# Turning the exponentials ahead of the new scores in the sixteen-pair attention

## The reference, cut to what matters

```
s = jnp.einsum('bqghd,bkgd->bghqk', qi, k_win).astype(jnp.float32) * scale
s = s - slopes * (t[:, None] - sp[None, :]).astype(jnp.float32)
p = masked_softmax(s, wmask)
o_win = jnp.einsum('bghqk,bkgd->bqghd', p.astype(dtype), v_win)
...
return g[..., 0:1] * o_cmp + g[..., 1:2] * o_slc + g[..., 2:3] * o_win
```

## Time and profile before

| | |
|---|---|
| time, median of 3 runs | 1466.04 us (1464.92 to 1466.94) |
| the profiled execution: time, span | 1466.22 us, 1464.4 us |
| PE busy | 1404.9 us (96%) |
| PEld, DVE, ACT, POOL busy | 1102.1, 593.2, 611.8, 626.4 us |
| mean granted TensorE clock | 0.988 |
| the sixteen-pair attention | about 558 to 703 us of the span |

### The profile page before, as it was taken

One profiled execution on the slowest core, in us unless ns is written; L12 is line 12 of the kernel. 1 busy time (PEld: TensorE's weight loads), 2 busy tenths in 40 slices (PEclk: granted clock), 3 DMA queues, 4 the chain that ended last, 5 costly groups with the idle time before them and its releaser, 6 DMA issues.

```text
span 1464.4 us, 19696 instructions
## 1 busy us (share of the span) xinstructions
PE 1404.9 (96%) x7313; PEld 1102.1 (75%) x7313; DVE 593.2 (41%) x1130; ACT 611.8 (42%) x1155; POOL 626.4 (43%) x345
## 2 busy tenths in 40 slices
PE   6999999999999999999999998898999999999999
PEld 5787887678778786666786687785788888888887
DVE  1104103732362244777343777978322332332000
ACT  4212222734123237888353665356343443443110
POOL 2763543564346523332335662520134444434441
PEclk9999999999999998999999999999999999999999
DMA  7553532012225420112123231102022323233230
GB/s 197 118 99 90 115 102 77 2 38 86 81 79 171 116 72 1 34 41 81 58 72 132 73 108 57 59 8 108 30 87 86 100 86 100 90 96 93 94 115 29
DMA packets 78399, 120.25 MB, mean 82 GB/s; under 512 B 8448, under 2 KB 41392, under 8 KB 77936
## 3 DMA queue, kind: packets, MB, share of 16 engines
q1 hardware_dynamic: 76096, 114.21, 26.9%
q0 software_dynamic: 2208, 4.98, 1.2%
q10 hardware_dynamic: 16, 0.00, 0.0%
HBM read 114.95 MB, written 4.19 MB: 81 GB/s over the span
## 4 chain that ended last, share of the span: by engine, by line
PE 77%; issue 8%; POOL 5%; DVE 3%; ACT 3%; DMA 2%; DVEq 1%; POOLq 1%; SPq 0%; ACTq 0%
PE psum L1685 20%; PE psum L1687 20%; PE psum L1686 20%; POOL weight_low L495 4%; PE psum L1734 3%; PE psum L1717 3%; PE psum L1697 3%; PE psum L1664 1%; PE psum L1845 1%; PE psum L2048 1%; PE psum L2024 1%; PE psum L1832 1%; ACT pair_probs L785 1%; POOL rstd L519 1%; DVEq L1412 1%
## 5 line engine op out<-in xcount | busy, mean ns | idle before, releaser
L495 POOL TENSOR_TENSOR weight_low<-weight_raw,weight_high 128x1024 fp32r<-128x1024 f32 x188 | 459.3, 2447 | 612.9 <-ACT weight_high L715 312.8
L1685 PE MATMUL psum<-act_ring,weight_high 128*128 128x512 f32 x704 | 282.8, 402 | 0.4 <-issue 0.4
L1687 PE MATMUL psum<-act_ring,weight_low 128*128 128x512 f32 x704 | 277.5, 394 | 0.0
L1686 PE MATMUL psum<-act_ring,weight_high 128*128 128x512 f32 x704 | 277.2, 394 | 0.0
L715 ACT ACTIVATE weight_high<-weight_raw 128x1024 fp32r<-128x1024 f32 x104 | 109.9, 1060 | 387.8 <-PE psum L1687 378.8
L1685 PE MATMUL psum<-weight_high,act_ring 128*128 128x512 f32 x480 | 193.4, 403 | 2.9 <-DVE odd_k L1292 2.3
L1687 PE MATMUL psum<-weight_high,act_ring 128*128 128x512 f32 x480 | 190.2, 396 | 0.0
L1686 PE MATMUL psum<-weight_low,act_ring 128*128 128x512 f32 x480 | 190.1, 396 | 0.0
L1685 PEld LDWEIGHTS psum<-act_ring,weight_high 128*128 128x128 f32 x704 | 132.6, 188 | 35.8 <-issue 5.2
L1687 PEld LDWEIGHTS psum<-act_ring,weight_low 128*128 128x128 f32 x704 | 132.4, 188 | 33.9
L1686 PEld LDWEIGHTS psum<-act_ring,weight_high 128*128 128x128 f32 x704 | 132.6, 188 | 30.7
(11 more groups left out here) (357 smaller groups left out, 2115.7 us busy)
## 6 DMA issues: line engine op xcount, KB each, us to landing
weight_raw<-in_w_ffn_in SPq DMA_DIRECT2D x88, 256.0 KB
weight_raw<-in_even_w_in SPq DMA_DIRECT2D x32, 512.0 KB
weight_raw<-in_w_in SPq DMA_DIRECT2D x24, 512.0 KB
weight_raw<-in_w_ffn_out SPq DMA_DIRECT2D x22, 512.0 KB
weight_raw<-in_odd_w_in SPq DMA_DIRECT2D x20, 512.0 KB
weight_raw<-in_even_w_out SPq DMA_DIRECT2D x8, 512.0 KB
weight_raw<-in_odd_w_in SPq DMA_DIRECT2D x16, 256.0 KB
weight_raw<-in_odd_w_out SPq DMA_DIRECT2D x8, 512.0 KB
```

Source lines behind the costliest of these rows:

```text
L495: nc.gpsimd.tensor_tensor(WL[:, r], RAW[:, r], WH[:, r].bitcast(f32), ALU.subtract).then_inc(split_ready, 1)
L1685: mm(bank, hi_l, hi_r, start=start, stop=False, skip_group_check=True)
L1686: mm(bank, hi_l, lo_r, start=False, stop=False, skip_group_check=True)
L1687: return mm(bank, lo_l, hi_r, start=False, stop=stop, skip_group_check=True)
```

## The change

In the loop of the sixteen-pair attention TensorE issues the turn of step u-2, with the one wait for `cmp_taken` that stands ahead of the first turn, before the scores of step u and no longer behind them. Nothing is added or taken away, and no other engine's order changes. The other two attentions of the kernel keep the old order.

```diff
             for u in range(ODD_UNITS + 4):
                 s = FOX_UNITS + u
+                if u == 2:
+                    pe.wait_ge(sem("cmp_taken"), 2 * NT)
+                if 2 <= u < ODD_UNITS + 2:
+                    pair_turn(s - 2)
                 if u < ODD_UNITS:
...
                     pair_scores(s, [part[:, 2 + q, :] for part in O_S], [part[:, b, :] for part in O_S])
-                if u == 2:
-                    pe.wait_ge(sem("cmp_taken"), 2 * NT)
-                if 2 <= u < ODD_UNITS + 2:
-                    pair_turn(s - 2)
                 if u >= 4 and u % 2 == 0:
```

## The result

The median of the changed kernel is 1509.9 us (1508.7 to 1510.1, four runs) and that of the kernel before, taken beside it, 1465.6: a ratio of 1.030 with a 95% interval of 1.028 to 1.032. The forecast was 1502.5 with a range of 1491 to 1517. The span of the profiled execution is 1508.2 us against 1464.4, so there are 43.8 us to place.

The account below looks back on a forecast made before the run. The stage was taken as bound by TensorE's amount of work. Loop stalls 33.2, first pair 2.0 and longer half-clock spell 1.2 sum to 36.4 us on 1466.22, forecast 1502.5; own range 1497 to 1509, 8 in 10 1491 to 1517.

Parts of the forecast that it names:

- The serial loop: Sixteen-pair attention: scores, DVE's maximum, copy of step s-2, turn, next scores; 2.25 us more a pair, 10.70 not 8.45.
- kind 0: Step with maximum 256 wide, copy 512: wait 1.36 us, 8 value matmuls cover 0.80, stall 0.56.
- kind 1: Step with maximum 128 wide, copy 384: wait 1.11 us, nothing for TensorE to do, stall 1.11.
- kind 3: Step with maximum 384 wide, copy 128: wait 1.10 us as measured, the back covers 0.52, stall 0.58.
- kind 2: Step with maximum 512 wide, copy 256: wait 1.37 us, 16 value matmuls take 1.67, no stall.
- The late back: Kind 3: back waits for ACT's pair copy, starts about 0.5 us late, ends about 1.04 behind scores, under the 1.10.
- The sign of failure: Forecast called wrong if, in kind 3, the back's wait for line 766 is the later one.
- The granted clock should stay 1.00 after the first pair: Stage's clock: no half clock beyond the start; only a longer first spell, taken as 1.2 us.
- rival 1: Clock falls in the stalls: 1.5 us lost per spell, 1515, 1527 or about 1600 us in all; chance 0.16.
- Is another engine late next? No.: Stage's other engines: DVE needs 6.3 us and ACT 7.0 a pair, both far under 10.7, so neither is late.
- Rival 2: Wait for the copy is shorter than summed, or only kind 1 stalls (18.7 us): time 1485; chance 0.10.
- Rivals 3 and 4: Turn ahead fills idle time, 2.2 us at most, 1464 (chance 0.02); or change does nothing, 1466 (chance 0.03).

Follow-up runs that it names:

- Experiment 1: Changed kernel, but in this stage DVE copies step s-2 ahead of the maximum of step s: 1476.9 us, ratio 1.007.
- experiment 4: Changed kernel plus 2, 4 and 2 products of zeros in steps of kind 0, 1 and 3, filling TensorE's idle places: 1502.0 us, ratio 1.025.
- Experiment 3: Changed kernel, but only head 1, whose bank ACT empties, is turned ahead of the scores, head 0 behind them: 1482.3 us, ratio 1.011.
- Experiment 7: Turn moved ahead of the scores only in steps of kind 3, otherwise the order of the kernel before: 1476.2 us, ratio 1.007.
- first version of the kernel before: Kernel before plus 5 and 8 products of zeros behind the scores of steps 0 and 1 of the sixteen-pair attention: 1465.9 us, ratio 0.9997.

## Why the prediction was right, and where it was off

**The serial loop.** Shown. The sum of maximum, copy and turn was right for each kind: from the end of the scores to the next turn it is 1.37 in kind 0 (1.36 forecast), 1.11 in kind 1 (1.11), 1.11 in kind 3 (1.10), and in kind 2 the values cover it. (The end is the next weight load in kind 0; in kinds 1 and 3, where TensorE idles, it is an estimate, the scores' first weight load plus their 0.48 and 0.72 of the earlier trace rows.) Experiment 1 cuts the loop at the one place that the forecast named, DVE's order, and 1.68 of the 2.22 us a pair go. With no more time at half clock than before, the stage costs 35.6 us more (experiment 4), against 33.2 + 2.0 forecast.

**The late back.** "About 0.5 late" was 0.52: it starts at 604.40 and the scores end at 603.88. It lies under the 1.11 as forecast, but only just: with its 0.52 of the earlier trace rows the back could end at 604.92, the copy ends at 604.87, and the turn starts at 604.99. The sign of failure that the prediction named, line 766 as the later wait in kind 3, stayed off by 0.07 us, and the chain even goes through line 766 there. So in kind 3 two paths end together. Some of the idle time also stands at another place than forecast: the waits view of TensorE's matmuls in the stage has 29.3 us ahead of line 1717 (its four rows added up, 33 forecast) and 6.0 ahead of line 1743.

**The clock.** Here the prediction was off, and by nearly all of the 7.4 us. "The granted clock should stay 1.00 after the first pair" is wrong: there are three spells in the pairs behind it. This is rival 1 in its mild form, and it is one of the signs by which the prediction called itself wrong. Together with the longer spell at the start they cost 4.2 us, where 1.2 was forecast. The term for what follows the stage was nothing, without a reason given, and it measured 4.0. The loop's own term was off by 0.4. That makes 3.0 + 4.0 + 0.4 = 7.4. Rival 1's price for one spell, 1.5 us, is about right for a spell in the full part: the pair with the spell at 588 took 12.26 us and not 10.67.

The Trainium skill, "TensorE: Matmul & The Clock Gate", section "A second HAM failure mode: psum-queue depth-cycling", says of a bf16 kernel that short idle moments between groups of matmuls let the clock swing back and forth. The trace agrees in part: the pairs have such idle moments throughout, but only three spells in sixteen pairs. With the moments filled (experiment 4) there is none behind the start.

**"Is another engine late next? No."** Right for the changed kernel, where DVE's loop hides nearly everything else, but too easy as an argument. It compared busy times with the period (7.0 us of ACT in 10.7) and put the need of head 1's exponential "more than 3 us" later. Experiments 1 and 3 show a second loop, through DVE's maxima, ACT's second exponential and ACT's copy; it costs 0.54 us a pair in the one and 0.84 in the other. Experiment 7 shows a third effect without any wait for a copy: scores that start 0.37 later push an exponential past the scores of kind 2.

**Rivals 2 to 4.** Rival 2 wanted the other kinds covered; kinds 0 and 3 wait as sized. Rivals 3 and 4 needed DVE's copy to be ready behind the values. Even with DVE copying first (experiment 1) the new order is 0.7% slower, and no run with a turn ahead of the scores came below the kernel before.

What stays open: an order of ACT and DVE that opens both loops without delaying an exponential wasn't found, and whether there is one isn't known. That the 4.0 us behind the stage are the clock is not shown by a run that holds it fixed, but the twelve profiles agree with it: with 10.2 and 13.7 us at half clock there, the rest of the kernel takes 761.4 and 761.5 us, with 20.5 (seven profiles) 763.6 to 764.2, and with 23.9 (three, the changed kernel among them) 765.5 to 765.8.

## What to carry to other kernels

When a piece is moved on one engine's queue, write down for each wait of that piece what stands ahead of the releasing instruction on the releasing engine's queue. If that needs the piece now put behind, a serial loop has closed, and its length can be read from rows where the loop already runs once, such as the end of the old loop. Then cut that loop on paper and look for the next one: where three engines fit each other to 0.05 us, as here, none of the swaps on one or two of them that were tried was a gain.

## What the runs showed of the hardware

The same idle moments were followed by a spell at half clock in one kernel and not in the other. TensorE's rows in the kernel before, with the idle time in brackets:

```profile
786.12 0.41 PE L2012 MATMUL psum<-identity,index_w_rows 8*128 8x8 f32 x4 [0.78 <-DVE index_w_rows L1389]
...
787.84 0.49 PE L2024 MATMUL psum<-index_k,index_q 64*128 64x256 f32 x2 [1.31 <-DVE index_w L1394]
```

and in the kernel after, with the windows before and behind them:

```profile
825.97 0.41 PE L2012 MATMUL psum<-identity,index_w_rows 8*128 8x8 f32 x4 [0.78 <-DVE index_w_rows L1389]
...
827.69 0.80 PE L2024 MATMUL psum<-index_k,index_q 64*128 64x256 f32 x2 [1.31 <-DVE index_w L1394]
```

```profile
823.50:827.30 3.80, 2.10 (x12) 1.07 (x10) 2.03 (x3) 0.00 (x0) 0.62 (x1) 0.99 0.48 149
827.30:834.00 6.70, 6.31 (x16) 4.67 (x17) 6.22 (x7) 2.57 (x6) 1.45 (x2) 0.50 0.09 39
```

Both kernels idle 0.78 and 1.31 us here. Before, the clock stayed at 1.00; after, it is 0.50 for 6.8 us, and line 2024 takes 0.80 and not 0.49. In the first version of the kernel before, which reaches this place 2.9 us earlier than its parent (783.18 and 786.12) with the same 0.78 and 1.31 us idle, it also fell. So a stage that starts at another moment can lose or win a few us in stages that weren't touched: behind this stage between 10.2 and 23.9 us were at half clock, and the rest of the kernel took 761.4 to 765.8 us. Nor did a full TensorE end a spell at once: in the kernel before, the clock stayed at 0.50 from 564 to 571.5 us, where TensorE was busy 7.47 of 7.50 us. Why the same gap is followed by a spell in one run and not in another wasn't found. A gain below some 4 us in one stage of this kernel has to be measured over the whole of it.
